# Eight stage boundaries of a two-block network on one core: filler products removed, a split in halves, transposes, a final piece and a factor row moved

## The reference, cut to what matters

```python
for i in range(DEPTH):                       # 4 layers: attention, short conv, conformer, attention
    a = rms_norm(h, mix_norm_pre[i])
    m = mixer(a)                             # attention | short_conv | conformer, first step a @ w_in
    h = h + rms_norm(m, mix_norm_post[i])    # <- boundary mixer -> FFN
    f = conv_ffn(rms_norm(h, ffn_norm_pre[i]), ffn_w_in[i], ffn_w_conv[i], ffn_w_out[i])
    h = h + rms_norm(f, ffn_norm_post[i])    # <- boundary FFN -> next mixer (or second block)
h = concat([meta_tokens, h])
h = h + 0.5 * swiglu(rms_norm(h, ffn1_norm), ...)   # second block, then attention and a second FFN

def rms_norm(x, g): return x * rsqrt(mean(x * x, -1) + 1e-6) * g
```

## Time and profile before

| what | value |
|---|---|
| median of 3 runs | 2247.0 us (2244.42 to 2250.31) |
| the profiled execution | 2244.87 us, its span 2243.1 us |
| TensorE busy (matmul) | 2167.7 us, 97% |
| VectorE, ScalarE, GpSimd busy | 67%, 45%, 21% |
| `keep_on` products | 48, the 42 in the trace 11.0 us busy |
| mean granted TensorE clock | 0.989 of full speed |

### The profile page before, as it was taken

How to read it: one execution, slowest core, us unless ns; L and a number is a source line. 1 busy time by engine, 2 the same in 40 slices (tenths; PEclk the granted TensorE clock), 3 DMA queues, 4 the chain that set the end, 5 groups by cost and what they waited for, 6 DMA issues and landing times.

```text
span 2243.1 us, 43438 instructions
## 1 busy us (share of the span) xinstructions
PE 2167.7 (97%) x16284; PEld 1997.6 (89%) x16307; DVE 1509.1 (67%) x2444; ACT 1012.3 (45%) x1363; POOL 472.8 (21%) x510
## 2 busy tenths in 40 slices
PE   6999999999999989999999999999999999989999
PEld 5998779988899878799889987899799999769999
DVE  6884768857688668588578748788465555645553
ACT  4334555544455443555443345555443343444342
POOL 2220004510135241045122200055023100100330
PEclk9999999999999999999999999999999999899999
DMA  5555225565545644245645551355645555104554
GB/s 168 181 181 187 74 101 169 187 202 179 197 150 186 203 146 134 75 166 183 199 157 185 187 187 39 110 185 184 216 132 176 171 178 178 38 1 145 182 185 145
DMA packets 299894, 350.27 MB, mean 156 GB/s; under 512 B 7494, under 2 KB 254940, under 8 KB 299804
## 3 DMA queue, kind: packets, MB, share of 16 engines
q1 hardware_dynamic: 298082, 347.07, 47.5%
q10 hardware_dynamic: 1466, 1.80, 0.2%
q0 software_dynamic: 256, 0.17, 0.0%
HBM read 346.34 MB, written 2.68 MB: 156 GB/s over the span
## 4 chain that ended last, share of the span: by engine, by line
PE 89%; DVE 5%; ACT 4%; issue 2%; DMA 0%; SPq 0%; ACTq 0%; DVEq 0%
PE ps L2042 25%; PE ps L2044 25%; PE ps L2043 25%; PE ps L2388 2%; PE ps L2359 1%; PE ps L2335 1%; ACT w_hi L1123 1%; PE ps L2346 1%; DVE w_lo L1506 1%; PE ps L2133 1%; PE ps L950 1%; DVE hstat L1583 1%; PE ps L2329 1%; PE ps L2128 0%; PE ps L2129 0%
## 5 line engine op out<-in xcount | busy, mean ns | idle before, releaser
L1506 DVE TENSOR_TENSOR w_lo<-raw,w_hi 128x2048 fp32r<-128x2048 f32 (+2 forms) x320 | 718.2, 2244 | 491.3 <-ACT w_hi L1123 491.2
L2042 PE MATMUL ps<-a_hi,w_hi 128*128 128x256 f32 (+1 forms) x3176 | 896.7, 282 | 1.3 <-DVE rope_cos L1551 0.5
L2044 PE MATMUL ps<-a_hi,w_lo 128*128 128x256 f32 (+1 forms) x3176 | 896.5, 282 | 0.0
L2043 PE MATMUL ps<-a_lo,w_hi 128*128 128x256 f32 (+1 forms) x3176 | 896.4, 282 | 0.0
L1123 ACT CAST w_hi<-raw 128x2048 fp32r<-128x2048 f32 (+2 forms) x320 | 591.6, 1849 | 566.3 <-PE ps L2044 550.7
L2042 PEld LDWEIGHTS ps<-a_hi,w_hi 128*128 128x128 f32 x3176 | 599.7, 189 | 3.3 <-DVE cv L1801 1.3
L2044 PEld LDWEIGHTS ps<-a_hi,w_lo 128*128 128x128 f32 x3176 | 600.4, 189 | 0.0
L2043 PEld LDWEIGHTS ps<-a_lo,w_hi 128*128 128x128 f32 x3176 | 597.0, 188 | 0.1
L1965 POOL TENSOR_TENSOR hs<-sg,cv 128x256 f32<-128x256 f32 x88 | 65.4, 744 | 694.7 <-DVE cv L1801 694.7
L1972 POOL CAST hid_hi<-hs 128x256 f32 (+3 forms) x132 | 140.0, 1061 | 322.0 <-DVE hs L1847 307.8
L2044 PE MATMUL ps<-w_hi,hid_lo 128*128 128x512 f32 x480 | 189.2, 394 | 0.0
(11 more groups left out here) (325 smaller groups left out, 2725.5 us busy)
## 6 DMA issues: line engine op xcount, KB each, us to landing
raw<-in_ffn_w_in_dram SPq DMA_DIRECT2D x88, 1024.0 KB, 5.1
raw<-in_attn_w_qkv_dram SPq DMA_DIRECT2D x72, 1024.0 KB, 5.0
raw<-in_ffn_w_out_dram SPq DMA_DIRECT2D x32, 1024.0 KB, 5.1
raw<-in_ffn_w_gate_dram SPq DMA_DIRECT2D x22, 1024.0 KB, 5.3
raw<-in_ffn_w_up_dram SPq DMA_DIRECT2D x22, 1024.0 KB, 5.4
raw<-in_ffn_w_down_dram SPq DMA_DIRECT2D x16, 896.0 KB, 4.7
raw<-in_sc_w_in_dram SPq DMA_DIRECT2D x12, 1024.0 KB, 5.1
raw<-in_ffn_w_out_dram SPq DMA_DIRECT2D x16, 768.0 KB, 4.4
```

What stands on the lines that cost most here:

```text
L1506: dve.tensor_tensor(o, src, hi.bitcast(F32), ALU.subtract).then_inc(lo_ready, 1)
L2042: pe.matmul(o, wh, xh, start=start, stop=False)
L2043: pe.matmul(o, wh, xl, start=False, stop=False)
L2044: return pe.matmul(o, wl, xh, start=False, stop=stop)
```

## The change

On TensorE, `keep_on(0)` takes away the 48 unread products. Transpose 3 stands behind the k = 0 products of tiles 0 and 1, with the wait for `gain(3)` in front of it. `spread_row` stands behind tile 2 instead of ahead of it (everywhere, the start of the program included). Tile 2 waits only for the first half of slab 1's low part, and for the other half at k = 4.

On VectorE, the low part of slab 1 is made in two halves of 128x1024: the first where the whole was (ahead of `gain(2)`), the second after the moments' aggregates. `gain(3)` and `residual(3)`, which stood behind the first and second `a_lo`, stand together behind the third. The four moments stand behind `a_lo` 3 to 6, the aggregates behind `a_lo` 7, and reciprocal and `spread` behind the second half.

On ScalarE, the root of the moments stands behind the last `a_hi`. On GpSimd, the diagonal matrices at boundary 4 wait for `row_ready` instead of `h_ready`.

```diff
@@ ScalarE, prenorm
                         if w == TW:
                             act.copy(h[:, k, :], turned_h(k, w)).then_inc(hT_ready, 1)
-                        if k == KD - 2:
-                            act.wait_ge(hms_ready, 2 * B["tok"] + 2)
-                            act.activation(hstd[:, 0:2], hms, ACT.Sqrt, bias=eps_rms).then_inc(hstd_ready, 1)
+                    act.wait_ge(hms_ready, 2 * B["tok"] + 2)
+                    act.activation(hstd[:, 0:2], hms, ACT.Sqrt, bias=eps_rms).then_inc(hstd_ready, 1)
@@ VectorE
+            def split_low_half(ph, half):
+                o, src, hi = (slab_view(t, ph, 1, ph.slot(1))[:, 4 * half:4 * half + 4, :] for t in (w_lo, raw, w_hi))
+                dve.wait_ge(hi_ready, ph.slab(1) + 1)
+                dve.tensor_tensor(o, src, hi.bitcast(F32), ALU.subtract).then_inc((lo_first, lo_ready)[half], 1)
...
                 if not is_last:
                     split_lo(ph, i + 1, 0)
+                elif ph.nxt is not None and ph.nxt.off:
+                    split_low_half(ph.nxt, 0)
...
@@ VectorE, prenorm behind a boundary (new order)
+                    else:
+                        for k in range(3):
+                            a_low(ph, k)
+                        gain(B["post"] - 1, 3)
+                        residual(B["post"] - 1, 3)
+                        for k in range(3, KD):
+                            a_low(ph, k)
+                            if k < KD - 1:
+                                dve.wait_ge(h_ready, 4 * B["post"] - 3 + (k - 3))
+                                moments(k - 3)
+                        mean_squares()
+                        split_low_half(ph.dense, 1)
+                        factors()
@@ GpSimd, cc_in
-                    pool.wait_ge(h_ready, 4 * B["post"])
+                    pool.wait_ge(row_ready, B["tok"])
@@ TensorE
-                            keep_on(5)
+                            keep_on(0)
...
-                            keep_on(3)
+                            keep_on(0)
...
-                        for k in range(2, 4):
-                            if n and k == 3:
-                                pe.wait_ge(out_gained, h0 + 4)
+                        for k in range(2, 3 if n else 4):
...
+                        if n and tok and k == 0:
+                            pe.wait_ge(out_gained, h0 + 4)
+                            turn_later(3)
...
+                            if ph.off and i is None and j == 2 and k == 4:
+                                slab_split(ph, 0, 1)
...
-                    if tok and w != TW:
+                    if ph.off:
+                        pe.wait_ge(lo_first, pre.base["post"])
+                    else:
+                        slab_split(ph, 0, 1)
+                    tile(None, 2)
+                    if tok:
                         spread_row()
-                    slab_split(ph, 0, 1)
-                    tile(0, 2)
-                    if tok and w == TW:
-                        spread_row()
-                    tile(0, 3)
+                    tile(None, 3)
```

More of the change, by code:

```diff
@@ L435, in build @@
         hi_half, lo_half = sem("hi_half"), sem("lo_half")
-        raw2_landed, hi2_ready, lo2_ready = sem("raw2_landed"), sem("hi2_ready"), sem("lo2_ready")
+        raw2_landed, hi2_ready, lo2_ready, lo_first = sem("raw2_landed"), sem("hi2_ready"), sem("lo2_ready"), sem("lo_first")
         tile_done, drained_a, drained_b = sem("tile_done"), sem("drained_a"), sem("drained_b")
@@ L1515, in split_ahead @@
                     split_lo(ph, i + 1, 0)
+                elif ph.nxt is not None and ph.nxt.off:
+                    split_low_half(ph.nxt, 0)
                 elif ph.nxt is not None:
-                    split_lo(ph.nxt, 0, ph.nxt.off)
+                    split_lo(ph.nxt, 0, 0)
             def split_second(ph, i):
@@ L1594, in mean_square_end @@
                                                  op0=ALU.mult, op1=ALU.add).then_inc(hms_ready, 1)
[L1596 to L1622, removed]
@@ new lines, in mean_squares, with factors @@
+                    def mean_squares():
+                        mean_square(0)
+                        mean_square(1)
+                        mean_square_end(0)
+                        mean_square_end(1)
+                    def factors():
+                        dve.wait_ge(hstd_ready, B["tok"] + 1)
+                        dve.reciprocal(rtok[:, 0:2], hstd[:, 0:2]).then_inc(rtok_ready, 1)
+                        dve.wait_ge(rtok_ready, B["tok"] + 1)
+                        for t in range(2):
+                            op = dve.tensor_scalar(spread[:, t, :], ident[:], rtok[:, t:t + 1], None, ALU.mult)
+                        if w != TW:
+                            op.then_inc(spread_ready, 1)
@@ new lines, in _ @@
+                    if ph.before is not None:
+                        for k in range(KD):
+                            a_low(ph, k)
+                    elif not n:
+                        dve.wait_ge(x_landed, 32)
+                        for k in range(KD):
+                            a_low(ph, k)
+                            if k < 4:
+                                moments(k)
+                        mean_squares()
+                        factors()
+                    else:
+                        for k in range(3):
+                            a_low(ph, k)
+                        gain(B["post"] - 1, 3)
+                        residual(B["post"] - 1, 3)
+                        for k in range(3, KD):
+                            a_low(ph, k)
+                            if k < KD - 1:
+                                dve.wait_ge(h_ready, 4 * B["post"] - 3 + (k - 3))
+                                moments(k - 3)
+                        mean_squares()
+                        split_low_half(ph.dense, 1)
+                        factors()
@@ L2080, in turn_later @@
                     def turn_later(k):
-                        if w == TW:
+                        if w == TW and k > 3:
                             pe.wait_ge(hT_ready, k - 3)
@@ L2165, in tile @@
                         c, slot = slice((j % 2) * P, (j % 2 + 1) * P), ph.slot(j // 2)
-                        bank_free(ph, i, j)
+                        bank_free(ph, 0 if i is None else i, j)
                         for k in range(KD):
+                            if ph.off and i is None and j == 2 and k == 4:
+                                slab_split(ph, 0, 1)
                             mm = mm3(ps[:, j, 0:w], w_hi[slot][:, k, c], w_lo[slot][:, k, c],
```

## The result

Over nine runs each the changed kernel took 2258.9 us (2256.2 to 2264.8) and the kernel before 2250.3: a ratio of 1.0041, 95% interval 1.0030 to 1.0053, or +9.2 us (the two medians differ by 8.6). The forecast was +5.3. The profiled execution took 2256.2 with a span of 2254.3 and a mean granted clock of 0.983; before, 2244.9, 2243.1 and 0.989. Both are near the lowest of their kernel's times, the changed one is the lowest of its nine, so other executions spent more time at the low clock than these two traces show.

What follows compares the result with a forecast made beforehand. Products set the pace inside stages, other engines between them, with fixed work behind ScalarE's table load. Terms without the clock sum to +0.1 us, lost clock cover adds +5.2: +5.3, median 2252, own range 2247 to 2257, whole range 2241 to 2260.

Steps and rivals of the forecast that it cites:

- boundaries 5, 7 (and 1): Boundaries where the half split does not bring the first `a_lo` forward, so the later table load costs +1.2 us each.
- 3, 6: Boundaries where the later table load (+1.2) is nearly offset by the half split (-1.1): +0.1 us each.
- 4: Boundary 4: with GpSimd's diagonal build behind `row_ready`, VectorE's small operations run alone: -3.3 us, between -2.5 and -4.1.
- start: Program start: the Sqrt table load moves behind the last `a_hi`: +0.5 us, between -0.3 and +1.3.
- conformer stage: Behind boundary 4: later load into the slab buffer off the path, build ending near 857, before taps at 862: no cost.
- unread products: Removing them lets the clock fall at boundaries 3 to 8: six times 0.87 us, +5.2, between 0 and 10.2.
- The chain behind the table load: FFN and attention boundaries: fixed 7.78 us follows the table load, which comes 8.18 us after first `a_lo`, not 6.99.
- the boundaries give what they seem to: Rival: TensorE's own shortening counts at the boundaries, about -12 us, or 2235 to 2240 with the clock fallen; chance 0.12.
- Boundary 8: Extra tokens' root and table load end about where they did, TensorE near them: -0.4 us, between 0 and -1.6.
- The list: Expected profile signs, among them PEclk 0.50 for 3.4 us or more at every boundary from 1 to 8.
- the clock holds: Rival: k = 0 products fill the gap and the clock stays up; sum +0.1 us, 2247; chance 0.18.
- it costs more: Rival: each boundary loses up to 1.71 us, not 0.87, deciding from 1.15; +12 us, 2259; chance 0.20.

Runs made afterwards that it cites:

- two of them were worth -7.4 us: Kernel before with GpSimd's build waiting for the row of factors and the second slab's low part in halves: 2242.5 us, ratio 0.9967.
- the moments first: Changed kernel, without products, VectorE's moments one chunk earlier so the aggregates stand ahead of the last two `a_lo`: 2248.9 us, ratio 0.9997.

## Why the prediction was right, and where it was off

The direction, the chain and most terms held; the sum was 3.9 us short, which the stated range (2241 to 2260) took in. Its own range of 2247 to 2257 and the chance of 0.54 for "within 0.3%" did not: the median is 2258.9. Of the 6.9 us from 2252 to there, 3.3 are the base, since the three runs of before (2247.0) lay under the nine (2250.3). The terms without the clock are read from the kernel with the products back against the kernel before. The start is the time to the last product ahead of boundary 1:

| term | forecast | measured |
|---|---|---|
| boundaries 5, 7 (and 1) | +1.2 each | +1.23, +1.24 (1: no pair with the same clock) |
| 3, 6 | +0.1 each | +0.26, +0.18 |
| 2 | -0.5 | -0.37 |
| 4 | -3.3 | -3.52 |
| 8 | -0.4 | +0.65 |
| start | +0.5 | -0.56 |
| conformer stage | 0 | +1.21 |
| sum of the timed runs | +0.1 | +2.5 (0.4 to 4.3) |
| unread products | +5.2 | +6.7 here, +5.2 in the order before |

**The chain behind the table load** was right in mechanism and size: 8.25 us against 8.18, the half split's 1.1 us at 3, 4, 6, 8 and none at 5 and 7, TensorE's own shortening worth nothing. The rival that the boundaries give what they seem to is refuted.

**Boundary 8** was mis-sized. The step that failed is "the extra tokens' root and table load end about where they did". ScalarE does the work on the extra tokens behind the root of the moments, and that root is now last and waits. First ScalarE's rows before, then those of the kernel with the products back:
```profile
1636.53 0.31 ACT L1168 ACTIVATE cols<-hstat,small 128x2 f32<-128x2 f32 x1
1637.16 0.49 ACT L1163 ACTIVATE a_hi<-ps,par 128x272 fp32r<-128x272 f32 x1 [0.32 <-PE ps L2072]
...
1639.31 1.28 ACT L674 ACT_TABLE_LOAD   x1
```
```profile
1641.19 0.49 ACT L1163 ACTIVATE a_hi<-ps,par 128x272 fp32r<-128x272 f32 x1 [0.52 <-PE ps L2091]
...
1643.17 0.30 ACT L1167 ACTIVATE cols<-hstat,small 128x2 f32<-128x2 f32 x1 [1.21 <-DVE hstat L1600]
...
1644.85 1.28 ACT L674 ACT_TABLE_LOAD   x1
```
Its table load is 1644.85 - 1632.86 = 11.99 us behind the first `a_lo`, 9.80 before, so 2.2 later. From the last `a_hi` to the table load it is 3.66 us, 2.15 before: 1.5 of the 2.2 is the root with its wait of 1.21. The other 0.7 is the last `a_hi` itself, 8.33 us behind the first `a_lo` instead of 7.65. The half split (-1.07) and a shorter third piece (-0.5) gave part back.

**The conformer stage** was put at nothing by two steps: the load behind the half split ("nothing is on the path") and the build that ends "ahead of the taps that need it". Each costs something when it is alone, 0.90 us for the half split with its later load and 0.55 for the moved build. The build overlaps the first low parts there, and TensorE waits 0.8 us for two of them in the changed kernel:
```profile
PE ps L2061 <- DVE w_lo L1505: 0.8, 2, 0.5
```
Boundary 8 and the conformer stage make 2.3 us more than forecast. The rows of the table, with boundary 1 at +1.2, add up to +1.5; the last us to the timed +2.5 is not placed, and the interval is wider than that. The start is not resolved either: in the six kernels that leave it alone its length ran from 318.7 to 320.1 us, and the -0.56 is less than that spread.

By the Trainium skill (SBUF — State Buffer, Who interferes with whom) the prediction estimated that the split of slab (1, 0) would lose up to 1.34 us to one GpSimd instruction. The trace does not show it at boundary 4: that split took its full 2.29 us here. It began at 826.22, 0.5 us ahead of the build, and whether that spared it was not tried. The next four, beside the build, took 2.31 to 3.02.

**The clock** was the right mechanism: products back, and most of the loss is gone. Its size came near in part by luck. The step "I take the price of boundary 1 for six: 6 x 0.87" gives the 5.2 that the products are worth in the order before, but not by six falls of 0.87. In the profile of that kernel the six boundaries lost 2.0, 0.2, 1.8, 1.3, 1.1 and 2.6 us, 9.0 together, most of them in stretches of 6.83 and not of 3.41; the timed runs gave 5.2, against a kernel before whose runs had on average more low clock than its profile (below). In the new order the products are worth 6.7, or 1.1 a boundary, which the intervals don't tell apart from 0.87.

The list said that the clock would be at 0.50 at every boundary; in the profiled execution it held at 1, 3 and 5. So the falls were fewer and each was dearer: against the kernel with the products back, boundary 7 lost 1.15 us in a stretch of 3.41, boundary 4 lost 1.3 in 3.41, 6 and 8 lost 1.9 and 1.6 in 6.83. That the clock holds is refuted. That it costs more, with its bound of 1.15 a boundary, came close without being shown. The Trainium skill (TensorE: Matmul & The Clock Gate, Part 4: PE-mode transpose) says that transposes do not count as busy the way products do. No run here tests transposes alone. The experiments fit it so far: with the same transposes in the gap, the clock fell at six of boundaries 3 to 8 without the eight full products in the order before, and at none with them.

The profiled execution of the changed kernel was 11.3 us over that of before. 3.9 of it came behind boundary 8, where a stretch at 2015.8 was at low clock for 20.5 us, 10.2 before; the timed runs of the kernel before spread by more than that by themselves (below).

## What to carry to other kernels

When an edit reorders the work between two stages, find the one instruction from which the rest is of fixed length (here a table load), and put ahead of it only what it needs: statistics before the last operands, not behind them. Work without a reader can be cover for the clock; before it is removed, price it by gaps where it is absent, and by more than one of them: here a boundary with the clock low lost from 0.2 to 2.6 us. Whether its worth depends on the order is not settled (6.7, 5.2 and 2.9 us in three orders, each with 2 to 3 us of noise). Try the parts of a bundle one by one: here two of them were worth -7.4 us, and the bundle +9.2.

## What the runs showed of the hardware

Most of the spread of the kernel before goes with the clock. In its 81 runs beside the experiments (2244.7 to 2254.0 us) I took twice (1 - mean granted clock) times the run's time as microseconds at 1.2 GHz. On average there were 63, about 16 more than in its profiled execution, and each one more came with 0.28 us of time (standard error 0.013, correlation 0.93): runs at a mean clock of 0.983 average 2253.2 us, those at 0.989 average 2245.3. By the same count, removing the products added 22 to 25 us at the low level (84 without them against 60 in the new order, 89 against 64 in the old, 82 against 60 with the moments first). At 0.28 us each that would be 6 to 7 us in every order, where 6.7, 5.2 and 2.9 were measured. So where a change costs cover, the mean granted clock of all timed runs shows that it does more surely than one profile, and the price still has to be timed.
